# Gated attention: gate products, softplus and log gates a head further ahead, and running sums between the masked copies of scores

## The reference, cut to what matters

```python
def gla_log_decay(h, w1, w2, b):
    z = ((h @ w1) @ w2 + b).astype(jnp.float32)
    return (jax.nn.log_sigmoid(z) / GLA_GATE_NORMALIZER).reshape(*h.shape[:-1], GLA_HEADS, GLA_DK)

def gla_chunked(q, k, v, g, s0):
    ...
    b = jnp.cumsum(gc, axis=2)
    b_last = b[:, :, -1:]
    q_dec = qc * jnp.exp(b)
    k_intra = kc * jnp.exp(-b)
    k_state = kc * jnp.exp(b_last - b)
    scores = jnp.where(mask, jnp.einsum('bnthd,bnshd->bnhts', q_dec, k_intra), 0.0)
    o_intra = jnp.einsum('bnhts,bnshv->bnthv', scores, vc)

    def step(S, xs):
        qd, ks, vv, bl = xs
        o = jnp.einsum('bthd,bhdv->bthv', qd, S)
        S = S * jnp.exp(bl)[..., None] + jnp.einsum('bthd,bthv->bhdv', ks, vv)
        return S, o
```

## Time and profile before

| what | value |
|---|---|
| median of three runs | 2866.8 us |
| the profiled execution | 2866.57 us |
| its span | 2864.8 us |
| PE busy | 2818.4 us, 98% |
| DVE busy | 1743.5 us, 61% |
| ACT busy | 1207.9 us, 42% |
| heads 0 to 3 in the trace | 247.67 to about 340.1 us |

### The profile page before, as it was taken

The page is one execution under the profiler, slowest core; times in us unless marked ns, Lnnn a source line. Parts: engine busy times, 40 slices in busy tenths (PEclk is TensorE's granted clock), DMA queues, the critical chain, the costliest instruction groups (busy, mean ns, idle before and its releaser), DMA issues.

```text
span 2864.8 us, 36836 instructions
## 1 busy us (share of the span) xinstructions
PE 2818.4 (98%) x14238; PEld 2362.5 (82%) x14238; DVE 1743.5 (61%) x2592; ACT 1207.9 (42%) x1858; POOL 59.0 (2%) x115
## 2 busy tenths in 40 slices
PE   8999999999999999999999999999999999999999
PEld 6998799999999976788888876588888765688887
DVE  5846758754674465447546469865365488765463
ACT  4235644321333384445334345653233455643231
POOL 0000000000000000000000010000000010000000
PEclk9999999999999999999999999999999999999999
DMA  7620023343432120022323231122222321123223
GB/s 289 234 89 30 1 95 123 127 129 105 126 127 71 59 75 16 1 78 96 105 87 101 91 114 64 30 85 99 93 98 103 103 86 42 52 96 105 88 101 104
DMA packets 73485, 266.16 MB, mean 93 GB/s; under 512 B 8816, under 2 KB 11376, under 8 KB 72032
## 3 DMA queue, kind: packets, MB, share of 16 engines
q1 hardware_dynamic: 63360, 230.31, 24.1%
q0 software_dynamic: 9952, 33.50, 3.4%
HBM read 253.55 MB, written 2.10 MB: 89 GB/s over the span
## 4 chain that ended last, share of the span: by engine, by line
PE 86%; DVE 6%; issue 5%; ACT 3%; DMA 0%; SPq 0%; ACTq 0%; DVEq 0%
PE psum L759 73%; DVE row_stats L1968 2%; DVE arena L1968 2%; PE psum L1131 2%; ACT temps L1408 2%; PE psum L1353 1%; PE psum L1291 1%; ACT arena L1408 1%; PE psum L1139 1%; PE psum L1159 1%; PE psum L853 1%; PE psum L852 1%; PE psum L854 1%; DVE temps L1968 1%; PE psum L1218 0%
## 5 line engine op out<-in xcount | busy, mean ns | idle before, releaser
L759 PE MATMUL psum<-arena_r,w_hi 128*128 128x512 f32 (+1 forms) x7416 | 2006.0, 369 | 3.0 <-DVE arena_r L1968 2.2
L759 PEld LDWEIGHTS psum<-arena_r,w_hi 128*128 128x128 f32 x7416 | 1336.9, 188 | 221.8 <-issue 61.9
L759 PE MATMUL psum<-arena_r,w_lo 128*128 128x512 f32 (+1 forms) x3708 | 1219.2, 364 | 0.0
L1968 DVE TENSOR_TENSOR w_lo<-w_raw,w_hi 128x1024 fp32r<-128x1024 f32 (+4 forms) x377 | 455.3, 1208 | 519.3 <-ACT w_hi L1408 518.8
L759 PEld LDWEIGHTS psum<-arena_r,w_lo 128*128 128x128 f32 x3708 | 682.4, 188 | 82.0
L1408 ACT ACTIVATE w_hi<-w_raw 128x1024 fp32r<-128x1024 f32 (+4 forms) x377 | 392.6, 1042 | 542.0 <-DMA w_raw<-in_weights 541.6
L1408 ACT ACTIVATE temps<-temps 128x512 f32<-128x512 f32 (+2 forms) x208 | 137.2, 662 | 154.5 <-DVE temps L1968 152.5
L1968 DVE SCALAR_TENSOR_TENSOR temps<-psum,vectors,temps 128x511 f32<-128x511 f32 x246 | 151.0, 655 | 62.9 <-ACT temps L1408 61.0
L1408 ACT ACTIVATE arena<-psum 128x768 f32<-128x768 f32 (+2 forms) x168 | 108.3, 649 | 168.6 <-PE psum L759 57.7
L1408 ACT ACTIVATE arena_r<-temps 128x512 fp32r<-128x512 f32 (+1 forms) x103 | 70.7, 687 | 143.5 <-DVE temps L1968 143.5
L1968 DVE TENSOR_TENSOR arena_r<-temps,arena_r 128x512 fp32r<-128x512 f32 (+1 forms) x103 | 78.2, 759 | 78.7 <-ACT arena_r L1408 78.7
(11 more groups left out here) (219 smaller groups left out, 2276.9 us busy)
## 6 DMA issues: line engine op xcount, KB each, us to landing
w_raw<-in_weights SPq DMA_DIRECT2D x261, 512.0 KB, 3.2
w_raw<-in_weights SPq DMA_DIRECT2D x64, 704.0 KB, 4.1
arena<-in_ada SPq DMA_DIRECT2D x32, 512.0 KB, 3.6
arena<-in_ada POOLq DMA_DIRECT2D x24, 512.0 KB, 4.6
modulation_weights<-in_ada POOLq DMA_DIRECT2D x24, 512.0 KB, 3.8
arena<-in_ada_first SPq DMA_DIRECT2D x8, 1024.0 KB, 18.9
w_raw<-in_weights SPq DMA_DIRECT2D x32, 256.0 KB, 2.6
modulation_weights<-arena POOLq DMA_DIRECT2D x60, 128.0 KB, 1.9
```

What stands on the lines that cost most here:

```text
L759: last = mm(lin_at(t, segs, slots, upper)[:, s:s + m], w[:, c], x(k, s, m), start=(k == 0 and a == 0), stop=(k == n_k - 1 and a == 2))
L1968: op(*args, **kw).then_inc(*C.out(signal))
```

## The change

It has four parts.

1. The gate product of head 1 is issued in the projection, after tile 22, and that of head h + 2 takes the place of that of head h + 1 in `gla_scores(h)`. Head 2 issues none. `softplus(1)` follows in ScalarE's stream after the r row of tile 22, between two table loads, and `log_gates(1)` in VectorE's ahead of the memset of the masks.
2. In the heads softplus and log_gates are those of head h + 2. The log gates stay somewhere else until they are summed: head 1's in two free areas, those of heads 2 and 3 where the queries and keys of heads 0 and 1 lay.
3. In heads 0 and 1 the two running sums of the next head stand in `masked`, one ahead of the first copy and one behind the second. In head 2 they stay between the updates.
4. In ScalarE's stream of every head `key_exponential(h + 1, 0)` and `query_exponential(h + 1, 0)` are now the first two, ahead of softplus and of `normed()`.

```diff
+        def log_gate(h, d):
+
+            if h == 0:
+                return key_gates(0, d)
+            if h == 1:
+                return (ADA_IN[:, 0:NT], SQSUM[:, :])[d]
+            return f_(QK0 + (h - 2 + 4 * d) * NT, NT)
...
                     decays(0)
+                if m == 21:
+                    pe.wait_ge(sems["z_taken"], 2)
+                    decays(1)
...
                         pe.wait_ge(*C.next("kt_made", 2))
-                        if h + 1 < GH:
-                            decays(h + 1)
+                        if h + 2 < GH:
+                            decays(h + 2)
...
-                    turn_out(h - 1, (sems["z_taken"], 2 * h + 4) if h + 1 < GH else C.at("kt_made"))
+                    turn_out(h - 1, (sems["z_taken"], 2 * h + 6) if h + 2 < GH else C.at("kt_made"))
...
+                if m == 22:
+                    load_set(LN_EXP_SET)
+                    softplus(1)
+                    load_set(SILU_SET)
...
             for h in range(GH):
                 if h + 1 < GH:
-                    softplus(h + 1)
+                    key_exponential(h + 1, 0)
+                    query_exponential(h + 1, 0)
+                if h + 2 < GH:
+                    softplus(h + 2)
                 if h:
                     normed()
-                if h + 1 < GH:
-                    key_exponential(h + 1, 0)
-                    query_exponential(h + 1, 0)
                 if h:
                     turned_out(h - 1, 0)
...
                 if t == 23:
+                    log_gates(1)
                     step(dve.memset, "dve_own", T[:, 0:2, :], 0.0)
...
                 for d in range(2):
+                    if not fill and d == 0:
+                        running_sum(h + 1, 0)
                     dve.wait_ge(*C.next("sc_done"))
...
                     if fill:
                         low(h - 2, d)
+                    elif d == 1:
+                        running_sum(h + 1, 1)
...
-                if ahead_of:
-                    log_gates(h + 1)
+                if h + 2 < GH:
+                    log_gates(h + 2)
                 update(h, 2)
-                if ahead_of:
+                if h >= 2 and ahead_of:
                     running_sum(h + 1, 0)
                 update(h, 3)
-                if ahead_of:
+                if h >= 2 and ahead_of:
                     running_sum(h + 1, 1)
```

More of the change, by code:

```diff
@@ L1579, in softplus @@
                 act.wait_ge(*C.next("z_done", 2))
-                to = [gla_tile(h, d) if h else key_gates(h, d) for d in range(2)]
+                to = [log_gate(h, d) for d in range(2)]
                 for d in range(2):
@@ L2220, in log_gates @@
                     dve.wait_ge(*C.next("l_made"))
-                    src = gla_tile(h, d) if h else key_gates(h, d)
-                    step(stt, "z_taken", key_gates(h, d), work(d), 0.0, src, ALU.min, ALU.subtract)
+                    step(stt, "z_taken", log_gate(h, d), work(d), 0.0, log_gate(h, d), ALU.min, ALU.subtract)
             def running_sum(h, d):
-                g, o = (x if d == 0 else x[:, NT - 1::-1] for x in (key_gates(h, d), gate_sums(h, d)))
+                g, o = (x if d == 0 else x[:, NT - 1::-1] for x in (log_gate(h, d), gate_sums(h, d)))
                 step(dve.tensor_tensor_scan, "b_made", o, CP[:, PC_SCAN:PC_SCAN + NT], g, 0.0, ALU.mult, ALU.add)
```

## The result

| what | before | after |
|---|---|---|
| median of nine runs | 2867.31 us | 2874.28 us |
| fastest and slowest of them | 2866.31, 2869.07 | 2873.16, 2875.42 |
| the profiled execution | 2866.57 us | 2875.06 us |
| its span | 2864.8 us | 2873.3 us |

The ratio is 1.0023 with an interval of 1.0014 to 1.0032, so the changed kernel is slower by 7.0 us. 2872.7 was forecast; the measured time is 1.6 us above it and inside the range.

What follows compares the result with a forecast made beforehand. PE was taken as the bound, busy 2818.4 of 2864.8 us, gains possible only where it waits; 1.50 - 1.45 - 0.30 - 0.15 - 0.65 + 5.70 - 0.15 + 1.4 = +5.9 gave 2872.7 us, range 2870.3 to 2875.0.

Steps and rivals of the forecast that it cites:

- gate product in the projection: Projection: head 1's four gate products on contiguous PE move everything after them later, +1.50 us.
- head 0, update no longer behind scans: End of head 0: with both scans out of the updates, the last update starts sooner, -1.45 us.
- head 1, clock stays up: Start of head 1: PE's 1.12 us idle gone, clock should stay up and scores(1) start sooner, -0.30 us.
- head 1, update no longer behind a scan: End of head 1: the last update no longer waits behind a scan after the last added(), -0.15 us.
- head 2, scores without gate product: Head 2: without a gate product the third group of scores is done sooner; step at the masked products -0.65 us.
- wait of turn_out(1): Head 2: PE's transposes of head 1's output wait for normed(), held behind an exponential awaiting head 3's first scan, +5.70 us.
- clock after it: Head 2, from turn_out(1): PE's clock falls in the wait and slows transposes and products behind it, +1.4 us.
- head 2, last update: End of head 2: the last update is no longer behind a scan, -0.15 us.
- the rival that rested on twice that: Projection: each new table load takes twice 1.28 us, leaving about 1.7 us on the path, 2874.4 us; chance 0.02.
- the 0.8 to 2 that the forecast allowed its case: Head 2: main case, wait comes with clock loss of 0.8 to 2 us, times 2872.1 to 2873.3; chance 0.60.
- the rival of the longer loss: Clock stays low into head 3's transposes and scores, +7.3 to +7.8 at most, 2874.3 us; chance 0.15.
- The upper bound of 3.0: Head 2: most the clock could cost, were it low through all work up to the last added(), 3.0 us.

Runs made afterwards that it cites:

- run 1: Kernel before, with only head 2's key and query exponentials of direction 0 moved ahead of normed(): 2875.66 us, ratio 1.0027.
- run 5: Changed kernel plus 24 extra unread products on PE in head 2's wait, before the transposes of head 1's output: 2872.59 us, ratio 1.0018.
- run 2: Changed kernel with head 2's two exponentials put back behind normed(): 2867.32 us, ratio 0.9997.
- run 3: Changed kernel with the first running sum of head 3 moved ahead of update 2 of head 2 on VectorE: 2869.83 us, ratio 1.0008.
- run 4: Changed kernel plus 48 extra unread products on PE in head 2, before the transposes of head 1's output: 2876.59 us, ratio 1.0032.
- run 6: Changed kernel with head 2's exponentials back behind normed(), plus two unread scans at the old places between head 0's updates: 2869.45 us, ratio 1.0006.
- the last run: Changed kernel with next head's key products between VectorE's updates, chunk ends and first scaled keys before update 4, ScalarE reordered: 2858.84 us, ratio 0.9971.

## Why the prediction was right, and where its sizes were off

In the profiled executions the changed kernel is late by 0.93 us already before its first changed instruction: the r row of tile 22 starts at 230.85, against 229.92. That is how two executions differ, not what the change does: run 1 has no edit ahead of head 2 and starts head 0 at 248.97 where the kernel before starts it at 247.67, 1.30 us later. Behind it, the shift of the same event by the two profiles, step by step:

| step of the sum | predicted | measured | from |
|---|---|---|---|
| gate product in the projection | +1.50 | +1.73 | r row of tile 23, 240.90 against 238.24, less 0.93 |
| head 0, update no longer behind scans | -1.45 | -1.44 | last update, 268.20 against 266.98 |
| head 1, clock stays up | -0.30 | +0.39 | last added(), 291.72 against 290.11 |
| head 1, update no longer behind a scan | -0.15 | -0.13 | last update, 292.78 against 291.30 |
| head 2, scores without gate product | -0.65 | -0.72 | third copies, 304.75 against 303.99 |
| wait of turn_out(1) | +5.70 | +5.72 | 318.44 against 311.96 |
| clock after it | +1.40 | +2.42 | added(), 322.73 against 314.13, and its 0.30 longer duration |
| head 2, last update | -0.15 | -0.11 | 324.11 against 315.32 |

The measured column comes to +7.9, with the 0.93 us to +8.8, and to +8.5 at the end of the span. The medians say +7.0: the profiled execution of the kernel before is 0.7 us below its median, that of the changed kernel 0.8 above. Two rows of the table have not stood here yet. The last update of head 2 before the change, on VectorE:

```profile
315.32 0.45 DVE L1968 SCALAR_TENSOR_TENSOR temps<-temps,chunk_decay,psum 128x256 f32<-128x256 f32 x1
```

and that of head 1 after it:

```profile
292.78 0.48 DVE L1983 SCALAR_TENSOR_TENSOR temps<-temps,chunk_decay,psum 128x256 f32<-128x256 f32 x1 [2.17 <-PE psum L951]
```

**The projection.** The gate product took 1.49 us start to start (230.75 to 232.24), with PE contiguous on both sides, as forecast. The step is 1.73 because the groups next to it are spaced wider too, start to start: 0.44 us ahead of it where such a group has 0.35, and 0.82 behind it where such a group has 0.69. The two table loads and six activations fit, by ScalarE's time line after:

```profile
231.68 1.28 ACT L1423 ACT_TABLE_LOAD   x1
232.98 0.81 ACT L1419 ACTIVATE modulation_weights<-psum 128x768 f32<-128x768 f32 x1
...
237.44 1.28 ACT L1423 ACT_TABLE_LOAD   x1
238.73 1.06 ACT L1419 ACTIVATE w_hi<-w_raw 128x1024 fp32r<-128x1024 f32 x1
240.90 0.81 ACT L1419 ACTIVATE arena<-psum 128x768 f32<-128x768 f32 x1 [1.10 <-PE psum L767]
```

1.10 us of idle time were left before the r row of tile 23, where 0.8 was forecast. The Trainium skill (ScalarE: Activation LUTs, What ACT_TABLE_LOAD costs) gives about 2.66 us for a switch of tables, in two parts, 1283 ns for the load itself and about 1380 ns for a drain; the prediction took the sum for the price of a load. The trace agrees with the first part, 1.28 us, and shows nothing of the second: the first new load starts 0.02 us after the end of the r row (230.85 + 0.81), and the next activation starts at 232.98, 0.02 us after the load's end. A switch cost 1.3 us here, and the rival that rested on twice that is out.

**Head 0.** Right. With a scan on each side of the first two copies, VectorE's wait for scores shrank from 3.5 us to 0.44:

```profile
253.24 1.75 DVE L1983 TENSOR_TENSOR_SCAN arena<-phase_constants,modulation_weights 128x768 f32<-128x768 f32 x1
254.91 1.32 DVE L1983 COPY_PREDICATED temps<-phase_constants,psum 128x512 f32<-128x512 int32 x2
256.12 1.74 DVE L1983 TENSOR_TENSOR_SCAN arena<-phase_constants,square_sum 128x768 f32<-128x768 f32 x1
258.30 0.78 DVE L1983 COPY_PREDICATED temps<-phase_constants,psum 128x256 f32<-128x256 int32 x2 [0.44 <-PE psum L935]
```

The first copy was late and nothing waited for it. Removing 3.3 us of scans from between the updates gave 1.45, because behind them stands the next bound, PE's own products.

**Head 1: the step that failed.** The prediction said that with the 1.12 us gone the remaining 2.17 stand alone and "the clock should stay up". It fell all the same: the transposes took 2.79 us, and the first scores behind them still 1.50 where such a group takes 1.13 at the upper level. The clock was low for as long as before, but later against the work. Before, it fell at about 270.1, 0.7 us ahead of the transposes, and was back at about 273.5, 2.7 us after their start; now it fell at about 272.1, as they started, and was back at about 275.6, 3.5 us after. So all of the low stretch lay in PE's work, where a part of it had lain in the wait. On PE's time line after:

```profile
274.64 1.50 PE L932 MATMUL psum<-arena 128*128 128x128 f32 x8
```

The reading of what PE had done before the fall, two waits close together, took a coincidence of one trace for its condition (last section). Here the clock fell with one wait only in front of it. This step was off by 0.7 us, and it made the kernel slower where a gain was forecast.

**Head 2's wait.** This was the term that decided, and it came within 0.02 us. Two exponentials took 1.48 us and normed() 3.1 us, in that order, behind a scan that no edit had moved. The first three runs show it from three sides: the edit alone makes it, its removal takes it away, an earlier scan shortens it.

**The clock behind the wait.** Right in kind, too small. The forecast took its size from head 1, 2.7 us low after the restart. Here the clock was low from about 316.5 to 323.3, and 4.9 us of that lay after the restart, through turn_out(1), carried(3) and the first half of the last added(): 2.4 us in the profile, 2.1 of it confirmed by filling the wait. Both are more than the 0.8 to 2 that the forecast allowed its case, and so is the time, 2874.3 against 2872.1 to 2873.3. The range holds it only because its upper end was set by the rival of the longer loss. That rival was right that the clock stays low longer, and it names the nearest time (2874.3 us), but by another way: it had the clock low into head 3, whose transposes in fact took 1.65 us. The upper bound of 3.0 held.

**The rest.** ScalarE's work behind turn_out(1) cost nothing, head 3 repeated, and the shift was carried to the end. Of the 1.6 us between forecast and median, 0.5 is the kernel before, whose nine runs have a median of 2867.3 where the forecast started from 2866.8. The shift itself is 7.0 against 5.9, 1.1 us more. In the profiled pair the steps come to 2.0 more than forecast, and the clock makes most of that: 0.7 in head 1 and 1.0 behind the wait, with 0.2 for the gate product. How the 1.1 us between the medians divide was not shown. Whether the kernel is slower by over 0.2%, which was given 0.53, is not decided either: the ratio is 1.0023, and its interval goes down to 1.0014.

## What to carry to other kernels

When an instruction is moved forward in a stream that can't reorder, ask in every iteration of the loop whether what it waits for moved with it; here it did in heads 0 and 1 and not in head 2, and the work behind it paid. A wait of the engine that bounds the kernel costs its length and, where its clock falls, its restart: here 5.57 us became about 8. Where filling the wait kept the clock up (run 5), 2.1 of it came back. Preparatory work of the next stage belongs between the handoffs of this one, ahead of the last handoff rather than behind it, so look for the operations that all stand after the last update before moving any that stand early.

## What was not expected of the hardware

The same wait before the next head's transposes (2.17 to 2.29 us, behind some 5 us or more of contiguous products, but for the 1.12 us where head 0 has them) sometimes leaves the granted clock at 1.00 and sometimes doesn't. By the duration of those 12 transposes in the one profiled execution of each kernel, 1.65 to 1.75 us at the upper level:

```
kernel          head 1   head 2   head 3
before           2.82     1.65     1.65
after            2.79     1.65     1.65
run 1            2.26     2.79     1.65
run 2            2.77     1.65     2.79
run 3            1.74     1.66     2.12
run 4            2.47     1.66     2.79
run 5            1.75     1.65     2.30
run 6            2.21     2.79     2.32
```

In 13 of 24 cases they took over 1.8 us, in 6 of 8 in head 1. Durations between 1.8 and 2.79 are falls that came after PE had work again, by up to 1.1 us: in run 6, head 1, the transposes start at 272.53 and the clock falls at about 273.6. Equal waits in equal code gave both results, so a single trace doesn't tell whether a wait of this length is free of a clock loss. What decides it was not found. In the last run, which has no wait above 1.1 us in heads 0 to 2, it was 1.00 throughout.
